# Gated linear attention of layer 0 set between the projection units of a two-layer diffusion block

## The chip, the cores and the metric

The kernel runs on one core of one Trainium2 chip, in one launch. The metric is the device time of that core in microseconds. Engines are named as in the profile: PE (TensorE), DVE (VectorE), ACT (ScalarE), POOL (GpSimd), SP (SyncE, which only issues transfers). Each engine runs its own instructions in the order written, and waits on semaphores for the others.

## The reference

Two transformer layers work on 512 tokens `x` and 256 context tokens `ctx` of width 1024, in float32. A conditioning vector gives six shift, scale and gate vectors for each layer (`silu(c) @ w_mod + b_mod`). Layer 0 has two mixers side by side:

```
aq, ak, av, bq, bk, bv, bo, rf, rb = split(h @ w_in)    # widths 512,128,128,256,256,512,512,16,16
log_f = log_sigmoid(rf @ gf_w + gf_b) / 16              # log_b likewise from rb
oa = window_attention(rope(aq), rope(ak), av, ...)      # 8 query heads, 2 key heads
ob = bidir_gla(bq * 64**-0.5, bk, bv, log_f, log_b)     # 4 heads, chunks of 64, both directions
y  = concat(oa, rms(ob) * norm_g * silu(bo)) @ w_out
# one direction of gla, per chunk:
cum = cumsum(log_a);  qg = q * exp(cum);  kg = k * exp(-cum)
o   = tril(qg @ kg.T) @ v + qg @ s_in
s   = exp(cum_last) * (s_in + kg.T @ v)                 # as the kernel arranges it
```

Then come a residual with gate and norm, a SwiGLU feed-forward (2816 wide) and its residual. Layer 1 has neighbourhood attention in place of the two mixers. Only `x` is returned.

## The kernel before, in words

**Precision.** Every large product is done in three passes of split float32: a weight tile `w` becomes `w_hi` (ACT, line 729) and `w_lo = w - w_hi` (POOL or DVE, line 454), the activations `h_hi` and `h_lo`, and PE adds hi*hi, hi*lo and lo*hi (`product3`, line 1451, and `tm_product`, line 1475). Small products are plain float32, and each of those matmuls shows as two records.

**Units.** `weight_units` lists all weights in the order in which PE uses them, 1024 columns at most to a unit. SP loads them into `w_raw` (3 places); ACT and POOL split them into rings of 3. ACT's and POOL's `feed(s)` split everything up to unit `s` at the place in their programs where it is written. An `fm_unit` is 24 passes over 512 and 256 columns with 128 output features on the partitions. `v0` (8 units, values for 6 token tiles) has the token on the partitions.

**Modulation.** A block of `w_mod` (one of 12 vectors) is eight rows of 512 KB. `modulation_rows` multiplies them (line 1519), ACT copies the result (`mod_copy`, line 738), PE turns it (`modulation_columns`, line 1532) and DVE adds the bias (`modulation`, line 1103). `modulation_plan` hangs the rows of blocks 2 to 5 on the projection units, three to a unit, and those of blocks 6 to 11 on feed-forward steps.

**Order on PE in layer 0.** `v0`; 14 projection units (four `a_q`, two `a_k` with each key head doubled, two `b_q`, two `b_k`, four `b_o`), with modulation rows between them; the first `scores` of attention; unit 14 (128 columns of which the 32 low-rank ones are used); window attention over 24 pairs of heads. After attention comes GLA, six token tiles and 12 chunks: `z` = low-rank times gate weights (line 1744), ACT's Abs, Exp and Ln, DVE's minimum (1290), running sums with a triangular matrix (1750), Exp twice (932, 933), products with `b_q` and `b_k` (1300, 1305), keys turned (1758), eleven state steps (1770 on PE, 1324 and 1328 on DVE), and for each tile scores (1784), masks (1341), outputs (1809, 1819), squares (718), root on POOL (625), norm (1367), turn (1795), gate (1352) and the split into `h_hi` and `h_lo`. Then `gate_rows(0, 2)` (1554) and the output product `out0L` (1475).

**Feed-forward.** `ffn_in` takes two units for each `j` of 11. ACT's part of step `j` is silu, a `feed`, `hid_hi`, a `feed`, the hook of `j`, then transfers of `w_mod` rows; PE's hook and modulation rows of step `j` stand behind its second unit.

Banks: `claim` makes PE wait for the readers of a PSUM bank, `read_by` names them.

Of the kernel before, what the change touches and what calls it, by code (L numbers as in the profile page):

```python
# [48 lines left out]
UNIT = 1024  # L49

# [35 lines left out]
def weight_units(a):  # L86
# [28 lines left out]
    for k in range(KT):  # L115
        tm(w, k, [(0, C_AV, AKV), (AKV, C_BV, BV)])
    begin("in0")
    parts = [[(0, C_AQ + j * P, P)] for j in range(4)]
    parts += [[(0, C_AK + 64 * j, 64), (64, C_AK + 64 * j, 64)] for j in range(2)]
    parts += [[(0, c + j * P, P)] for c, n in ((C_BQ, 2), (C_BK, 2), (C_BO, 4)) for j in range(n)]  # L120
    parts += [[(0, AB_IN - P, P)]]
    for part in parts:
        fm(w, part)
    rows("out0L", a["ab_w_out"][0], range(KT))
    rows("out0C", a["ab_w_out"][0], range(KT))
# [23 lines left out]
FENCE = 2600  # L149


def modulation_plan(start):
# [12 lines left out]
    spread("in0", range(11), 2 * KT, 6 * KT, lambda i: start["in0"] + i if i else start["v0"] - 2, 5)  # L165
    half = [start["fi0L", h] for h in range(2)]
    spread(("fi0L", 0), range(4, 10), 6 * KT, 8 * KT, lambda j: half[0] + 2 * j, 5)
# [41 lines left out]
def build(nc, a, out):  # L209
# [23 lines left out]
    with ExitStack() as ctx:  # L233
# [12 lines left out]
        with ExitStack() as early:  # L246
            sb("before", [P, D], scope=early)

            rel = sb("rel", [P, 2, 8, BIAS_RUN], scope=early)
        with ExitStack() as early:  # L250
            sb("before_mask", [P, 4 * D + 4 * P], scope=early)
            mask0 = sb("mask0", [P, 7 * P], scope=early)
# [5 lines left out]
        near_b = sb("near_b", [P, LT, 2 * P], BF16)  # L258
        tri = sb("tri", [P, 2, P])
# [21 lines left out]
        with ExitStack() as s0:  # L281
            par_rows = sb("par_rows", [P, 2, P], scope=s0)
            mask_in = sb("mask_in", [P, LT * 2 * P], scope=s0)
        with ExitStack() as s1:
            b_q = sb("b_q", [P, 2, TOK], scope=s1)
            b_k = sb("b_k", [P, 2, TOK], scope=s1)
            b_v = sb("b_v", [P, NT, BV], scope=s1)
            b_o = sb("b_o", [P, 4, TOK], scope=s1)
            r_t = sb("r_t", [33, TOK], scope=s1)
            gw = sb("gw", [33, 2 * BQK], scope=s1)  # L290
            with ExitStack() as s2:
                with ExitStack() as s3:
                    sb("fence1", [P, FENCE], scope=s3)
                    mod_early = sb("mod_early", [P, MOD_RING, UNIT], scope=s3)
                rope = sb("rope", [P, 4, SEQ], scope=s2)
                cos, sin, rope_t = rope[:, 0], rope[:, 1], rope[:, 2:4]
                a_q = sb("a_q", [P, 4, TOK], scope=s2)
                a_k = sb("a_k", [P, 2, TOK], scope=s2)
                a_v = sb("a_v", [P, NT, AKV], scope=s2)
                prob0 = sb("prob0", [P, 2, 2, 5 * P], scope=s2)  # L300
            with ExitStack() as s2:
                with ExitStack() as s3:
                    la = sb("la", [P, NT, 2 * BQK], scope=s3)
                kg_t = sb("kg_t", [P, NT, 2 * BQK], scope=s2)
                qg = sb("qg", [P, 4, TOK], scope=s2)
                kg = sb("kg", [P, 4, TOK], scope=s2)
                att_m = sb("att_m", [P, 2, 4 * P], scope=s2)
# [8 lines left out]
        with ExitStack() as s1:  # L316
# [6 lines left out]
            on1 = sb("on1", [P, 2 * P], scope=s1)  # L323
# [15 lines left out]
        mod_landed = [sem(f"mod_landed{i}") for i in range(MOD_RING + MOD_HOLD)]  # L339
        (consts_in, par_in, x_in, gw_zero, gw_in, rel_in, stored) = map(sem, (  # L340
            "consts_in", "par_in", "x_in", "gw_zero", "gw_in", "rel_in", "stored"))
        gl_av = sem("gl_av")
# [13 lines left out]
        at_b, v_mixed, mask0_in = sem("at_b"), sem("v_mixed"), sem("mask0_in")  # L356
# [36 lines left out]
        def in0_bank(i):  # L393

            return 4 if i == 14 else 2 * (i % 2)

# [8 lines left out]
        def mod_slot(m):  # L405

            if m < 2 * KT:
                return m % MOD_RING
            return MOD_RING + m % MOD_HOLD if m >= 6 * KT else MOD_RING - MOD_HOLD + (m - 2 * KT) % MOD_HOLD

        def mod_place(m):
            n = mod_slot(m)
            return mod_raw[:, n - MOD_RING, :] if n >= MOD_RING else mod_early[:, n, :]
# [17 lines left out]
        mod_first = set(range(2 * KT))  # L431
        mod_next = {}
        for phase in ("in0", ("fi0L", 0), ("fi0L", 1), "fi0C"):
            at = sorted(i for name, i in mod_hooks if name == phase)
            mod_first |= set(mod_hooks[phase, at[0]])
            mod_next |= {(phase, i): mod_hooks[phase, j] for i, j in zip(at, at[1:])}

        def row_place(b):

            return gate_b[:, b % 2, 0:256] if b < 6 else mod_row[:, b % 2, :]  # L440

        def mod_bank(b):
            return 6 + b % 2

        def column_bank(b):
            return b if b < 2 else 4 + b % 2
# [114 lines left out]
        def _(sync):  # L561
# [14 lines left out]
            for u, parts in enumerate(units):  # L576
                if u == sp("v0") + RAW:
                    for m in range(12, 2 * KT):
                        mod_load(sync, m)
                    for dst, src in ((mask_in[:], a["k_near"]), (tri[:].rearrange("p a n -> p (a n)"), a["k_tri"]),  # L580
                                     (cos, a["k_cos"]), (sin, a["k_sin"])):
                        sync.dma_start(dst, src).then_inc(consts_in, 16)
                if u == sp("in0") + 6:
                    sync.wait_ge(pre_lo, PRE["mix0"] + NT)
                    sync.dma_start(mask0[:], a["k_window"]).then_inc(mask0_in, 16)
# [6 lines left out]
                for layout, at, width, src in parts:  # L592
                    dst = w_raw[:, u % RAW, :]
# [13 lines left out]
        def _(pool):  # L607
# [30 lines left out]
            feed(sp("in0") + 14)  # L638
            for t in range(NT):
                root(gla_ssq[:, t, :], gla_ms[:, t, :], gla_rs[:, t, :], P, t, gl_ssq, gl_ms, gl_rs, 4)  # L640
            feed(sp("out0C") + RING - 2)
# [68 lines left out]
        def _(act):  # L710
# [169 lines left out]
            for t in range(NT):  # L880
                wait_tm(act, "v0", t, KT)
                act.activation(b_v[:, t, :], ps(t, 0, BV), ACT.Copy).then_inc(v_act, 1)

            def in0_unit(i):
                s = sp("in0") + i
                feed(s + RING - 2)
                act.wait_ge(w_used, s + 1)
                bl = in0_bank(i)
                bc = bl + 1
                lat, con = ps(bl, 0, SEQ), ps(bc, 0, CTX)  # L890
                if i == 6:
                    act.wait_ge(masks_done, 1)
                if i < 6:
                    dst = a_q[:, i] if i < 4 else a_k[:, i - 4]
                    act.activation(dst[:, SEQ:], con, ACT.Copy).then_inc(fe_act, 1)
                    return
                if i < 8:
                    dst, fn, scale = b_q[:, i - 6], ACT.Copy, SCALE
                elif i < 10:
                    dst, fn, scale = b_k[:, i - 8], ACT.Copy, 1.0  # L900
                elif i < 14:
                    dst, fn, scale = b_o[:, i - 10], ACT.Silu, 1.0
                else:
                    dst, fn, scale = r_t[0:32], ACT.Copy, 1.0
                    lat, con = ps(bl, 0, SEQ, 96, P), ps(bc, 0, CTX, 96, P)
# [3 lines left out]
            for i in range(14):  # L909
                in0_unit(i)  # L910
                if i in (3, 6, 8, 11):
                    mod_copy({3: 2, 6: 3, 8: 4, 11: 5}[i])
                for m in mod_next.get(("in0", i), ()):
                    mod_load(act, m)
            feed(sp("in0") + 14)
            attention(0, lambda: in0_unit(14))


            for t in range(NT):
                act.wait_ge(gl_z, t + 1)  # L920
# [1007 lines left out]
```

## Time and profile before

| | us |
|---|---|
| median of 3 runs (1890.68 to 1891.32) | 1890.8 |
| profiled execution | 1891.36 |
| its span, first to last instruction | 1889.6 |
| PE busy | 1751.4 |
| ACT, POOL, DVE busy | 660.2, 596.8, 547.1 |
| mean granted clock of PE | 0.967 of full |

Busy times are of one profiled execution. A granted clock of 1.0 is 2.4 GHz, 0.5 is 1.2 GHz; a figure between is a mean over a stretch. A timeline row gives the start, how long the group lasts, the engine, line, output and inputs, the count, and in brackets how long the engine was idle before it and what ended that.

### The profile page before, as it was taken

How to read it: one execution, taken by the hardware profiler on the slowest of the kernel's cores; microseconds unless marked ns; L12 is line 12 of the kernel's file. 1: busy time of each engine (PE TensorE's matmuls, PEld its weight loads, DVE VectorE, ACT ScalarE, POOL GpSimd, SP SyncE). 2: the span in 40 equal slices, each digit the busy share in tenths (PEclk: the TensorE clock that was granted, in tenths of full speed). 3: DMA queues.
4: the chain of work that ended last, by engine and by line, in shares of the span. 5: the costliest groups of instructions: out<-in, count | busy, mean ns of one | idle time of the engine just before them, and what ended most of it. 6: DMA issues, size and time to landing. Idle time of an engine off the chain costs nothing.

```text
span 1889.6 us, 26709 instructions
## 1 busy us (share of the span) xinstructions
PE 1751.4 (93%) x10718; PEld 1439.8 (76%) x10718; DVE 547.1 (29%) x1057; ACT 660.2 (35%) x1145; POOL 596.8 (32%) x426
## 2 busy tenths in 40 slices
PE   4899999777999999999999999999999799999996
PEld 2788877466777778777789887887787588788875
DVE  2221047641442101100376542002773411011103
ACT  3321256512453212222255434223773432222221
POOL 1222200013753343334230005332543344444442
PEclk8899999779999999999999999999999799999998
DMA  8246400002336424652465663623101133333331
GB/s 332 55 147 209 145 13 2 1 2 64 107 97 206 151 90 145 198 173 92 156 183 148 180 190 89 121 81 123 35 2 34 45 93 98 93 97 96 94 99 57
DMA packets 208150, 204.97 MB, mean 108 GB/s; under 512 B 10950, under 2 KB 179356, under 8 KB 208028
## 3 DMA queue, kind: packets, MB, share of 16 engines
q1 hardware_dynamic: 195064, 162.25, 28.6%
q10 hardware_dynamic: 12964, 41.01, 6.8%
q8 instruction: 86, 1.41, 0.3%
q14 instruction: 36, 0.29, 0.0%
HBM read 201.14 MB, written 2.10 MB: 108 GB/s over the span
## 4 chain that ended last, share of the span: by engine, by line
PE 63%; DVE 3%; ACT 2%; issue 2%; POOL 1%; DVEq 0%; ACTq 0%; POOLq 0%
PE ps L1451 34%; PE ps L1475 22%; PE ps L1612 2%; PE ps L1668 2%; PE ps L1633 2%; PE ps L1519 1%; ACT w_hi L729 1%; DVE x_res L513 1%; POOL w_lo L454 1%; DVE x_res L1080 0%; DVE full L1052 0%; DVE w_lo L454 0%; PE ps L1554 0%; ACT junk L718 0%; DVE h_lo L1058 0%
## 5 line engine op out<-in xcount | busy, mean ns | idle before, releaser
L454 POOL TENSOR_TENSOR w_lo<-w_raw,w_hi 128x1024 fp32r<-128x1024 f32 (+1 forms) x203 | 482.3, 2377 | 916.1 <-ACT w_hi L729 915.9
L1451 PE MATMUL ps<-h_hi,w_hi 128*128 128x512 f32 (+1 forms) x1520 | 505.7, 352 | 18.1 <-DVE w_lo L454 8.6
L1451 PE MATMUL ps<-h_hi,w_lo 128*128 128x512 f32 (+1 forms) x1520 | 500.9, 349 | 0.0
L1451 PE MATMUL ps<-h_lo,w_hi 128*128 128x512 f32 (+1 forms) x1520 | 499.8, 348 | 0.0
L729 ACT ACTIVATE w_hi<-w_raw 128x1024 fp32r<-128x1024 f32 (+1 forms) x277 | 288.9, 1044 | 382.8 <-PE ps L1475 363.3
L1451 PEld LDWEIGHTS ps<-h_hi,w_hi 128*128 128x128 f32 x1520 | 275.5, 190 | 70.2 <-issue 25.8
L1451 PEld LDWEIGHTS ps<-h_hi,w_lo 128*128 128x128 f32 x1520 | 275.2, 190 | 37.4
L1451 PEld LDWEIGHTS ps<-h_lo,w_hi 128*128 128x128 f32 x1520 | 275.1, 190 | 36.4
L454 DVE TENSOR_TENSOR w_lo<-w_raw,w_hi 128x1024 fp32r<-128x1024 f32 x74 | 98.6, 1332 | 270.6 <-ACT w_hi L729 270.4
L1135 DVE TENSOR_TENSOR hid_f<-silu_g,ps 128x512 f32<-128x512 f32 (+1 forms) x66 | 39.4, 597 | 398.3 <-PE ps L1451 398.0
L1475 PE MATMUL ps<-w_hi,hid_hi 128*128 128x512 f32 x440 | 138.3, 395 | 8.1 <-ACT mod_row L738 3.0
L1475 PE MATMUL ps<-w_hi,hid_lo 128*128 128x512 f32 x440 | 137.9, 395 | 0.0
L1475 PE MATMUL ps<-w_lo,hid_hi 128*128 128x512 f32 x440 | 137.9, 394 | 0.0
L790 ACT ACTIVATE hid_hi<-hid_f 128x512 fp32r<-128x512 f32 (+1 forms) x66 | 36.9, 560 | 249.7 <-DVE hid_f L1135 249.7
L1475 PE MATMUL ps<-w_hi,h_hi 128*128 128x512 f32 (+1 forms) x352 | 107.0, 386 | 15.6 <-POOL w_lo L454 5.0
L1475 PE MATMUL ps<-w_lo,h_hi 128*128 128x512 f32 (+1 forms) x352 | 105.3, 381 | 0.0
L1475 PE MATMUL ps<-w_hi,h_lo 128*128 128x512 f32 (+1 forms) x352 | 105.1, 381 | 0.0
L1475 PEld LDWEIGHTS ps<-w_hi,hid_hi 128*128 128x128 f32 x440 | 82.5, 188 | 28.6 <-issue 9.6
L1475 PEld LDWEIGHTS ps<-w_lo,hid_hi 128*128 128x128 f32 x440 | 82.9, 188 | 19.4
L1475 PEld LDWEIGHTS ps<-w_hi,hid_lo 128*128 128x128 f32 x440 | 82.9, 188 | 19.3
L786 ACT ACTIVATE silu_g<-ps 128x512 f32<-128x512 f32 (+1 forms) x66 | 34.5, 523 | 168.6 <-PE ps L1451 168.5
L1475 PEld LDWEIGHTS ps<-w_hi,h_hi 128*128 128x128 f32 x352 | 66.4, 193 | 30.7 <-issue 12.9
(179 smaller groups left out, 1695.0 us busy)
## 6 DMA issues: line engine op xcount, KB each, us to landing
w_raw<-in_w_ffn_in SPq DMA_DIRECT2D x132, 512.0 KB, 3.8
w_raw<-in_w_ffn_out SPq DMA_DIRECT2D x66, 512.0 KB, 3.6
mod_raw<-in_w_mod ACTq DMA_DIRECT2D x39, 512.0 KB, 5.1
w_raw<-in_na_w_in SPq DMA_DIRECT2D x32, 512.0 KB, 3.7
mod_early<-in_w_mod ACTq DMA_DIRECT2D x29, 512.0 KB, 4.7
mod_early<-in_w_mod SPq DMA_DIRECT2D x19, 512.0 KB, 10.4
w_raw<-in_ab_w_out SPq DMA_DIRECT2D x16, 512.0 KB, 3.6
w_raw<-in_ab_w_in SPq DMA_DIRECT2D x13, 512.0 KB, 4.1
```

The source lines that it names most:

```text
L454: eng.tensor_tensor(w_lo[:, u % RING, 0:width], w_raw[:, u % RAW, 0:width], w_hi[:, u % RING, 0:width].bitcast(F32), ALU.subtract).then_in ...
L513: eng.tensor_tensor(x_res[:, t, :], x_res[:, t, :], post_place(name, i), ALU.add).then_inc(post_x, 1)
L729: act.activation(w_hi[:, u % RING, 0:width], w_raw[:, u % RAW, 0:width], ACT.Copy).then_inc(w_hi_done, 1)
L786: act.activation(silu_g[:, f % 2, 0:width], ps(2 * (f % 2), 0, width), ACT.Silu)\
L790: act.activation(hid_hi[:, j * width:(j + 1) * width], hid_f[:, f % 2, 0:width], ACT.Copy)\
L1135: dve.tensor_tensor(hid_f[:, f % 2, 0:width], silu_g[:, f % 2, 0:width], ps(2 * (f % 2) + 1, 0, width), ALU.mult).then_inc(ff_full, 1)
L1451: mm = pe.matmul(o[0], sta(x, o), mov(y, o), start=first and n == 0, stop=last and n == 2)
L1475: mm = pe.matmul(o, act(x, k, t), w[y][:, c:c + n], start=k == 0 and (x, y) == ("hi", "hi") and first_in_bank(name, i, c), stop=k == n_uni ...
L1519: mm = pe.matmul(ps(bank, 0, 256, 32 * g, 32 * g + 32), c_pad[:, k, :], mod_place(m)[:, 256 * g:256 * g + 256], start=k == 0, stop=k == KT ...
L1612: mm = pe.matmul(ps(scores_bank(layer, p, x), at, at + width), q, kk[:, col:col + width], start=at % 512 == 0, stop=i == len(runs[x]) - 1, ...
L1633: mm = pe.transpose(ps(4 + x, j * P, (j + 1) * P), probs(p, x, j), ident[:])
L1668: mm = pe.matmul(ps(bank, at, at + P, 64 * x, 64 * x + 64), value_tile(p, x, j), turned_probs(layer, p)[:, x, j * P:(j + 1) * P], start=j ...
```

## The change

GLA runs between the projection units, in place of after attention. `projection_steps()` gives the list; PE carries out the steps of a slot behind the unit's last matmul. Unit order, low-rank columns, head pairing, buffers and banks follow from that.

```diff
+def projection_steps():
+    rows = {(0, 0): 3, (0, 1): 3, (1, 0): 2, (1, 1): 2, (2, 0): 2, (2, 1): 2, (3, 0): 2}
+    steps, m = {}, 3 * KT
+    for at, n in rows.items():
+        steps.setdefault(at, []).append(("rows", list(range(m, m + n))))
+        m += n
+    for at, names in {
+            (0, 0): (("z", 2), ("z", 3), ("columns", 2)), (0, 1): (("z", 4), ("z", 5)),
+            (1, 1): (("cum", 0), ("cum", 1), ("columns", 3)), (2, 0): (("cum", 2), ("cum", 3), ("cum", 4)),
+            (2, 1): (("cum", 5), ("kt", 0), ("kt", 1)), (3, 0): (("kt", 2), ("kt", 3), ("kt", 4)),
+            (3, 1): (("kt", 5), ("columns", 4)), (4, 0): (("ds", 0), ("ds", 1)), (4, 1): (("ds", 2), ("ds", 3)),
+            (5, 0): (("ds", 4), ("ds", 5)), (5, 1): (("ds", 6), ("ds", 7)), (6, 0): (("ds", 8), ("ds", 9)),
+            (6, 1): (("ds", 10), ("scores", 0))}.items():
+        steps.setdefault(at, []).extend(names)
+    steps = {(i, 1): steps.get((i, 0), []) + steps.get((i, 1), []) for i in range(7)}
+    for t in range(NT):
+        steps[7 + t, 1] = [("turn", t - 1)] if t else []
+        steps[7 + t, 1] += [("out", t)] + ([("scores", t + 1)] if t + 1 < NT else [])
+    return steps
...
-        tm(w, k, [(0, C_AV, AKV), (AKV, C_BV, BV)])
+        tm(w, k, [(0, C_AV, AKV), (AKV, AB_IN - 2 * RANK, 2 * RANK), (VR, C_BV, BV)])
...
+    parts = [[(0, c + j * P, P)] for c, n in ((C_BK, 2), (C_BQ, 2), (C_BO, 4)) for j in range(n)]
+    parts += [[(0, C_AK, P)]]
+    parts += [[(0, C_AQ + 64 * j, 64), (64, C_AQ + 64 * (j + 4), 64)] for j in range(4)]
...
-    spread("in0", range(11), 2 * KT, 6 * KT, ...)
-    spread(("fi0L", 0), range(4, 10), 6 * KT, 8 * KT, lambda j: half[0] + 2 * j, 5)
+    spread(("fi0L", 0), range(3, 11), 5 * KT, 8 * KT, lambda j: half[0] + 2 * j, 5)
...                                             # PE
+            pe.wait_ge(r_out, 2)
+            claim(2, 6)                         # then six tiles of r_tok turned into r_t
...
+            modulation_rows(range(2 * KT, 3 * KT))
...
+            gla_z(0)
+            gla_z(1)
+            for i in range(13):
+                bl = 2 * (i % 2)
+                claim(bl, bl + 1)
+                fm_unit(sp("in0") + i, [(ps(bl, 0, SEQ), 0, SEQ), (ps(bl + 1, 0, CTX), SEQ, CTX)],
+                        middle=lambda: in0_step(i, 0))
+                read_by((bl, bl + 1), (fe_act, i + 1), *([(fe_dve, i - 7)] if i >= 8 else []))
+                in0_step(i, 1)
             gla_turn(NT - 1)
+            pe.wait_ge(rope_done, 5)
+            attention(0, lambda first: first())
...                                             # PE, a state step: order of the loops
-                for m in range(4):
-                    for hh in range(2):
+                for hh in range(2):
+                    for m in range(4):
...                                             # PE, first feed-forward half
-                                             8: lambda: modulation_columns(6)}, "ffn0L")
+                                             6: lambda: modulation_columns(5), 9: lambda: modulation_columns(6)},
...                                             # ACT
+            for i in range(13):
+                feed(sp("in0") + i + 2)
+                if i == 1:                      # six Exp, six Ln, then
+                    mod_copy(3)
+                if i == 2:
+                    gla_decay(2)
+                    gla_decay(3)
+                    gla_decay(4)
+                if i == 3:
+                    mod_copy(4)
+                for m in in0_later.get((i, 0), ()):
+                    mod_load(act, m)
+                in0_unit(i)
+                if i >= 7:
+                    gla_square(i - 7)
+                if i == 1:
+                    gla_decay(0)
+                    gla_decay(1)
+                if i == 2:
+                    gla_decay(5)
+                for m in in0_later.get((i, 1), ()):
+                    mod_load(act, m)
...
-                   {3: ..., 7: lambda: mod_copy(6), 10: lambda: mod_copy(7)})
+                   {3: ..., 6: lambda: mod_copy(5), 9: lambda: mod_copy(6), 10: lambda: mod_copy(7)})
...                                             # POOL
-            feed(sp("in0") + 14)
             for t in range(NT):
+                feed(sp("in0") + 9 + t)
                 root(gla_ssq[:, t, :], ...)
+            pool.wait_ge(w_used, sp("out0L"))
+            for t in range(NT):                 # h_hi and h_lo of the GLA half, from b_o
+                pool.wait_ge(gl_full, t + 1)
+                pool.tensor_copy(h_hi[:, 4:8, cols], b_o[:, :, cols]).then_inc(gl_hi, 1)
+                pool.tensor_tensor(h_lo[:, 4:8, cols], ..., ALU.subtract).then_inc(gl_lo, 1)
...                                             # DVE, after the state steps
+            for t in range(NT):
+                if t:
+                    rotate(7 + t)
+                    gla_gate(t - 1)
+                if t + 1 < NT:
+                    gla_mask(t + 1)
+                gla_norm(t)
+                if t == 0:
+                    gla_gain(3)
+            gla_gate(NT - 1)
+            attention(0)
```

A slot is what stands between two units; the transposes of the keys (`kt`) begin in the slot behind unit 2. `z` uses banks 4 and 5 in turn, `cum` banks 4, 5, 4, 5, 6, 4, `kt` banks 5, 6, 4, 5, 6, 4, the state steps 4 to 7, scores 4 and 5, outputs 6 and 7, turns 4; projection units use banks 0 to 3. DVE replaces ACT's Abs by two operations on `z` (the minimum, and twice the minimum less `z`). SP loads rows 16 to 23 of `w_mod` ahead of unit 5 of `v0`, rows 24 to 33 ahead of the weights of projection units 1 and 3, and the rotation tables ahead of unit 11; ACT loads rows 34 to 39. Query heads `j` and `j + 4` now share a unit, so `a_k` needs one unit, and the rows of `ab_w_out` are loaded in that order, in two transfers for each of the first four units. The whole window mask is loaded with the other constants and held in bfloat16.

## Rows read from the trace of the kernel before

**Rows 1.** The page, part 1: busy us, share of span, instructions of PE.
```profile
PE 1751.4 (93%) x10718; PEld 1439.8 (76%) x10718; DVE 547.1 (29%) x1057; ACT 660.2 (35%) x1145; POOL 596.8 (32%) x426
```

**Rows 2.** View by stretches: from:to length, busy by engine, PEclk, DMA share, GB/s.
```profile
108.90:248.20 139.30, 138.25 (x946) 111.82 (x945) 21.15 (x47) 25.71 (x41) 31.10 (x13) 1.00 0.53 165
...
256.70:336.30 79.60, 76.94 (x809) 57.22 (x808) 56.30 (x197) 56.04 (x160) 0.00 (x0) 1.00 0.01 2
336.30:443.50 107.20, 70.87 (x654) 55.76 (x653) 53.69 (x140) 32.21 (x87) 9.04 (x13) 0.72 0.00 1
...
370.00:387.00 17.00, 11.92 (x174) 8.18 (x168) 14.91 (x40) 0.00 (x0) 0.00 (x0) 0.50 0.00 1
```

**Rows 3.** PE's waits, 100 to 450: total us, times, longest.
```profile
PE ps L1809 <- DVE b_q L1352: 7.9, 3, 2.8
```

**Rows 4.** Timeline of PE: attention's last matmuls, and the first of `out0L`.
```profile
335.72 0.64 PE L1680 MATMUL ps<-ident,sm 128*64 128x128 f32 x8
...
449.90 0.70 PE L1475 MATMUL ps<-w_hi,h_hi 128*128 128x512 f32 x2 [1.63 <-ACT gate_b L776]
```

**Rows 5.** Timeline, end of `v0` and projections: PE, VectorE, ScalarE.
```profile
107.84 0.50 PE L1475 MATMUL ps<-w_hi,h_hi 128*128 128x128 f32 x2
108.18 0.50 PE L1475 MATMUL ps<-w_lo,h_hi 128*128 128x128 f32 x2
...
109.06 1.28 DVE L1263 COPY a_v<-ps 128x128 f32<-128x128 f32 x6 [36.09 <-PE ps L1475]
...
117.43 1.50 PE L1519 MATMUL ps<-mod_early,c_pad 128*32 128x256 f32 x24
...
237.41 0.60 ACT L906 ACTIVATE b_o<-ps 128x512 f32<-128x512 f32 x1 [6.39 <-PE ps L1451]
...
245.96 0.60 ACT L906 ACTIVATE b_o<-ps 128x512 f32<-128x512 f32 x1 [6.72 <-PE ps L1451]
```

**Rows 6.** Timeline of the GLA stretch: ScalarE and PE.
```profile
344.42 0.60 ACT L923 ACTIVATE la<-ps 128x512 f32<-128x512 f32 x1 [0.45 <-PE ps L1744]
...
346.12 0.60 ACT L923 ACTIVATE la<-ps 128x512 f32<-128x512 f32 x1 [0.45 <-PE ps L1744]
...
348.69 3.78 ACT L928 ACTIVATE la<-la,one_col 128x512 f32<-128x512 f32 x6
...
350.19 3.61 PE L1750 MATMUL ps<-tri,la 128*128 128x128 f32 x16 [4.11 <-DVE la L1290]
...
357.26 2.14 PE L1750 MATMUL ps<-tri,la 128*128 128x128 f32 x16 [0.19 <-ACT kg L933]
...
400.88 2.05 PE L1809 MATMUL ps<-b_v,att_m 128*128 128x128 f32 x16
402.86 1.16 PE L1819 MATMUL ps<-state,qg 64*64 64x128 f32 x32
...
404.71 1.16 PE L1784 MATMUL ps<-qg,kg 64*128 64x128 f32 x16
```

**Rows 7.** Timeline of PE: one of the state steps, eight alike.
```profile
378.32 1.15 PE L1770 MATMUL ps<-b_v,kg_t 64*64 64x128 f32 x16 [0.50 <-DVE state L1324]
```

**Rows 8.** Timeline of PE: the last output and the last turn.
```profile
436.73 1.97 PE L1819 MATMUL ps<-state,qg 64*64 64x128 f32 x24
...
442.62 1.09 PE L1795 MATMUL ps<-ident,b_k 128*128 128x128 f32 x4 [3.27 <-DVE b_k L1367]
```

**Rows 9.** Timeline, start of attention: PE and ScalarE.
```profile
246.97 1.13 PE L1612 MATMUL ps<-a_k,a_q 64*128 64x256 f32 x8 [1.05 <-ACT b_o L907]
...
250.49 0.71 ACT L819 ACTIVATE prob<-prob,negm 128x512 f32<-128x512 f32 x1
...
256.71 1.13 PE L1612 MATMUL ps<-a_k,a_q 64*128 64x256 f32 x8
```

**Rows 10.** Timeline, end of the first feed-forward half: ScalarE and PE.
```profile
661.38 0.36 ACT L738 ACTIVATE mod_row<-ps 128x256 f32<-128x256 f32 x1
...
662.10 0.71 PE L1475 MATMUL ps<-w_hi,hid_hi 128*128 128x512 f32 x2 [2.96 <-ACT mod_row L738]
```

More of the change, by code:

```diff
@@ L220, in unit_width @@
     def unit_width(u):
-        return sum(width for _, _, width, _ in units[u]) * (KT if units[u][0][0] == "fm" else 1)
+        return sum(width for layout, _, width, _ in units[u] if layout != "bottom") * (KT if units[u][0][0] == "fm" else 1)
     def sp(name):
@@ L291, in build @@
+            a_v = sb("a_v", [P, NT, AKV], scope=s1)
             with ExitStack() as s2:
[L292 to L298, printed above, removed]
@@ L951, in _ @@
+            attention(0, lambda: None)
             gate_rows(0, 2)
@@ new lines, in _ @@
+            modulation(4)
+            dve.wait_ge(fe_act, 4)
+            dve.wait_ge(gl_dec, NT)
+            for n in range(NT):
+                cols = slice(GLA_TILES[n] * P, (GLA_TILES[n] + 1) * P)
+                for d in range(2):
+                    last = dve.tensor_tensor(qg[:, 2 * d:2 * d + 2, cols], qg[:, 2 * d:2 * d + 2, cols],
+                                             b_q[:, :, cols], ALU.mult)
+                last.then_inc(gl_q, 1)
+            for i in range(2 * NT - 1):
+                gla_state(i)
+                if i in (4, 8):
+                    gla_gain(i // 4 - 1)
@@ L1737, in _ @@
-            pe.wait_ge(rope_done, 6)
-            attention(0, lambda first: (first(), in0_unit(14)))
-            pe.wait_ge(gw_in, 64)
-            claim(*range(8))
-            for t in range(NT):
-                pe.matmul(ps(t, 0, 512), r_t[:, t * P:(t + 1) * P], gw[:], start=True, stop=True).then_inc(gl_z, 1)
-                read_by((t,), (gl_la, t + 1))
-            for t in range(NT):
-                claim(6 + t % 2)
-                pe.wait_ge(gl_la, t + 1)
+            read_by((6, 7), (v_dve, 2))
@@ L1822, in _, with gla_turn, in0_step @@
                 mm.then_inc(gl_o, 1)
-                read_by((ob, ob + 1), (gl_on, t + 1))
-                if t:
-                    gla_turn(t - 1)
+                read_by((6, 7), (gl_on, t + 1))
+            def gla_turn(t):
+                pe.wait_ge(gl_on, t + 1)
+                claim(4)
+                for h in range(4):
+                    mm = pe.transpose(ps(4, h * P, (h + 1) * P), gla_on[:, t % 2, h * P:(h + 1) * P], ident[:])
+                mm.then_inc(gl_f, 1)
+                read_by((4,), (gl_full, t + 1))
+            gla = {"z": gla_z, "cum": gla_cum, "kt": gla_keys, "ds": gla_change, "scores": gla_scores, "out": gla_out,
+                   "turn": gla_turn, "rows": modulation_rows, "columns": modulation_columns}
+            def in0_step(i, half):
+                for name, x in in0_steps.get((i, half), ()):
+                    gla[name](x)
+            gla_z(0)
+            gla_z(1)
+            for i in range(13):
[5 more added lines that the diff above has]
+                in0_step(i, 1)
             gla_turn(NT - 1)
+            pe.wait_ge(rope_done, 5)
+            attention(0, lambda first: first())
             gate_rows(0, 2)
```

465 lines of the change are left out of this document (244 added, 221 removed).

## The prediction, made before the result was known

> **What bounds the kernel now.** I read the page first: TensorE (PE) is busy 93% of the span [rows 1]. The reader should see there that only time in which PE waits, or work taken from PE, can shorten the kernel. The view by stretches then shows where PE waits [rows 2]. In the projections (108.9 to 248.2) PE is busy 138.25 of 139.3 us while VectorE has 21 us and ScalarE 26 us of work. In the stretch of gated linear attention (GLA, 336.3 to 443.5) PE is busy 70.87 of 107.2 us at a mean granted clock of 0.72. That is the only stage ahead of the feed-forward part with both a large gap and a low clock. The list of PE's waits names its gaps, the longest in total VectorE's `b_q` with 7.9 us in three times [rows 3]. They are the links of one dependent chain (logarithm, running sum, transpose, states, output), which nothing else covers. So the limit of that stage is latency, and the limit of its neighbour is PE.
>
> **The sum's frame.** I cut the profiled execution where the order of work changes. It took 1891.4 us, 1.8 more than its span of 1889.6. The median of the runs is 1890.8, so 0.6 less; a difference worked out on the first is carried to the second.
>
> **1. The stretch after attention goes.** Attention's last matmul for a norm ends at 336.36, and `out0L` starts at 449.90 [rows 4]: 113.5 us. Afterwards only `gate_rows(0, 2)` stands between them, 32 records of 128 columns. Such records take some 0.13 us each at the high clock (16 in 2.05 or 2.14 [rows 6]), so about 4.2. The wait for ScalarE's second gate copy, 1.63 us [rows 4], stays. Attention's last `h_lo` lies beside this. 113.5 - 5.8 = **107.7 us removed**. The GLA split of `h_hi`/`h_lo` moves from ScalarE and VectorE to GpSimd during attention, where GpSimd has no work at all in 79.6 us [rows 2]: six copies and six subtractions at no more than a `w_lo` subtraction of twice the size (13 in 31.10 us, 2.4 each [rows 2]) are under 29 us. Nothing if that cover holds; if it ran past the end, `out0L` would wait for it.
>
> **2. What the projections become.** From `v0`'s last matmul (108.86) to the second `scores` of attention (256.71) it is 147.85 us now [rows 5, 9]. The new PE program, term by term:
> - 13 units instead of 15. ScalarE's copies start at 237.41 and 245.96 [rows 5]: 8.55 us a unit. 13 x 8.55 = 111.2.
> - 24 modulation rows (blocks 2 to 4; block 5 leaves). Three of them take 1.50 us [rows 5]; with the change of shape I take 0.52 a row: 12.5. Eight stand bare before unit 0, sixteen in the slots behind units 0 to 3. Three transposes of columns: 0.8.
> - The low-rank columns. VectorE must copy banks 6 and 7 (four copies) before PE can turn them. `a_v` alone took 1.28 us in six copies [rows 5]; I take 1.7 of wait, bounds 0.5 and 2.5. Six matmuls of two records: 1.5. Together 3.2.
> - GLA's matmuls at the high clock. `z`: 1.70 us apart at the low clock (ScalarE's readers) [rows 6], half of that at the high one, 6 x 0.85 = 5.1. Running sums: 2.14 for two tiles, 6.4 in all. Transposes of `kg`: 24 records of 0.13, 3.1. Scores: 1.08 each, 6.5. Outputs: 1.98 + 1.08, two of them shorter, 18.0. Five turns of 0.6: 3.0. Total 42.1 [rows 6].
> - The eleven state steps. PE needs 1.15 us for one at a granted clock of 0.50 [rows 2, 7], so between 0.55 and 1.1 at the high one; the reordered loop changes row halves more often and column halves less, and no row shows what that does. With its wait of 0.50 for VectorE the step is 1.65 long [rows 7]: VectorE's pace, some 0.8 for each of its two halves. Four steps in a slot: PE's fourth must wait for VectorE's second sum, 0.6 + 0.1 + 3 x 0.8 = 3.1, then 0.65: 3.75 us. If a step cost 1.1, it would be 4.7. The slot behind unit 6 has three steps and the first scores, which need VectorE's last sum: 4.7 ahead of them. I take 3.75 + 3.75 + 4.7 = 12.2, bounds 11 and 15.
> - Waits in the slots. Behind unit 0, `z` 4 and 5 reuse banks 4 and 5 and wait for VectorE, which first does the modulation columns and then two passes a tile: 1.2 us. Behind unit 1 there is none: ScalarE's six Exp and six Ln (3.78 us for six [rows 6]) with two changes of table between them end some 15 us after unit 0, and the first running sum is wanted at 18.5. Behind unit 2, `cum` 5 and `kt` 0 and 1 reuse banks which ScalarE's two Exp a tile (about 1.0) free in 3.4, 4.4 and 5.5 us, while PE comes to them at 5.3, 6.4 and 6.9. That is where turning one unit later pays: keys 2 to 5 need VectorE's 1.6 us a tile. Behind unit 8 the third scores need `gla_gate(0)`, queued on VectorE behind `rotate` (six of them are most of VectorE's 21.15 us in the projections [rows 2], so under 3.5; I take 2.8): ready at 3.7, wanted at 3.7. 1.0 for what I miss: 2.2.
> - 13 changes of shape at 0.1: 1.3.
> - The tail. After the last output PE waits for the squares, GpSimd's root and VectorE's norm: 438.70 to 442.62, 3.9 us [rows 8]. Then turn 0.75, scores 1.13, and the first softmax, which unit 14 covered: scores end at 248.1 and the second Exp ends at 251.2 [rows 9]. Now PE meets that wait, about 1.9 us more than the unhindered order, and 1.5 for a lower clock after the pause (the turn at 442.62 took 1.09 us, 0.27 a record where 0.13 is the high clock's). 3.9 + 0.75 + 1.13 + 1.9 + 1.5 = 9.2.
>
> Sum 111.2 + 12.5 + 0.8 + 3.2 + 42.1 + 12.2 + 2.2 + 1.3 + 9.2 = 194.7, against 147.85: **46.8 us added**.
>
> **3. v0.** 32 more columns in 144 matmuls. A 512 and a 128 take 0.34 us together [rows 5]; a 512 and a 256 take 8.55 / 24 = 0.356. So 128 columns more cost 0.017, 32 of them 0.004: 0.6 us, and 0.2 for GpSimd's wider `w_lo`: **0.8 added** (bounds 0 and 2). SP's eight loads of block 2 come between the weights of `v0` units 4 and 5, which are wanted much later. The six loads issued behind `mod_used` hold up unit 3's weights on SP, which are not wanted for some 30 us.
>
> **4. The first feed-forward half.** Block 5's eight rows go there: 4.2, of which three rows fall into a wait that is there already, so 2.5. Then the hooks: PE turns columns 5 at `j` = 6 and columns 6 at `j` = 9, and ScalarE copies the row to be turned in its hook of the same `j`, behind silu's partner, `hid_hi` and a `w_hi`. The trace has this order once, at the end of the half: `mod_row` is copied from 661.38, and PE goes on at 662.10 after 2.96 us of wait [rows 10]. Twice that is 5.9. Bounds: 0 if ScalarE came early, which its in-order queue excludes, and 6.5. The columns 0.25, and 0.5 for rows whose loads ScalarE issues only after `pre_high`. **9.2 added.** The two records after that wait took 0.71 us, so no clock was lost in it.
>
> Total: -107.7 + 46.8 + 0.8 + 9.2 = **-50.9**. 1891.4 - 50.9 = 1840.5; on the medians **1840**.
>
> The clock is where the Trainium skill speaks against the change. The row: 370 to 387, short state matmuls between waits of 0.5 us ran at 0.50 of the full clock (1.2 GHz) [rows 2, 7]; attention, with matmuls as small but few waits, at 1.00 [rows 2]. The Trainium skill (TensorE: Matmul & The Clock Gate, section "HAM oscillation — how this bites in real kernels") says that bursts of matmuls parted by waits throw the engine back to the lower clock each time. By it every slot would start low, the third rival; by the attention row it would not, and the sum stands.
>
> **Rivals.**
> - *The waits come along.* PE's 36.3 us of gaps [rows 2] are not hidden but land in the slots, because a slot holds several dependent steps and PE is in order. For: slots 0 and 2 are tight. Against: the dependent steps stand a whole unit (8.55) apart. Two fifths of them would be 15 us: 1855.
> - *Cheaper.* The low-rank wait, the waits in the slots, the slow clock in the tail and part of the state chain are not met, and the column waits shrink: -9: 1831. For: all were taken at or above the middle. Against: the 2.96 was measured.
> - *Lower clock, slower than before.* The granted clock falls at each slot. The slots' 42.1 us of small matmuls then take up to 1.7 times as long (3.61 against 2.14 for two tiles [rows 6]), +29, the rows and states +8, and some 4 us at the head of each of 13 units run at half pace, +26: 1840 + 63 = 1903. It decides from about 50 us, that is, only if nearly all slots fall. Against: PE would be busy almost without a gap from 68 to 336.
> - *The chain slips a slot.* ScalarE holds `feed` behind a wait for PE, and a unit starts without its weights. A `w_hi` (1.06) and `w_lo` (2.4) after the late wait is 3.7 us, in eight units 30: 1870. Against: weights are fed two units ahead.
>
> **How the numbers follow.** Forecast 0.58, its own range 1834 to 1848; waits 0.19; cheaper 0.15; slipping chain 0.05; low clock 0.03. The range of 8 in 10 takes the forecast, most of the cheap case and the middle of the waits: 1832 to 1858. A measurement tells 0.2% (3.8 us) from no change: faster 0.96, within 0.2% 0.01, slower 0.03.
>
> **What would show it.** Right: 13 units of 8.55 us and slots of 3 to 8 us between them, clock 1.00 through `v0`, projections and attention; `out0L` about 6 us after attention; two new waits of about 3 us for `mod_row` at `j` = 6 and 9; a pause of about 4 us before the last turn. Wrong: waits over 2 us in the slots behind units 1 to 5, a clock below 1.00 there, a wait for `w_lo` at a unit's start, or `out0L` waiting for GpSimd.

## The result, and the profile after

The changed kernel takes 1860.0 us (median of 4 runs, 1858.07 to 1861.23); the kernel before took 1891.1 beside it. The ratio is 0.9835, 95% interval 0.9818 to 0.9852. I forecast 1840 with a range of 1832 to 1858: the direction was right, the gain of 51 us was 31, and the time lies above the range.

The view by stretches of the changed kernel (from:to length, busy us by engine, PEclk, DMA share, GB/s):

```profile
109.20:117.40 8.20, 6.80 (x81) 4.26 (x81) 3.02 (x8) 1.83 (x3) 0.38 (x1) 1.00 0.36 112
117.40:230.00 112.60, 100.30 (x771) 80.02 (x771) 51.54 (x115) 32.16 (x51) 19.20 (x8) 0.94 0.35 100
230.00:306.00 76.00, 72.12 (x634) 63.31 (x632) 29.50 (x61) 17.58 (x61) 18.85 (x17) 1.00 0.14 36
306.00:311.60 5.60, 3.13 (x13) 1.94 (x13) 2.87 (x8) 0.07 (x1) 5.36 (x7) 0.50 0.00 0
311.60:392.70 81.10, 78.88 (x808) 58.67 (x808) 57.49 (x198) 56.71 (x162) 5.73 (x7) 0.97 0.01 2
392.70:399.20 6.50, 3.84 (x33) 3.71 (x33) 0.88 (x3) 3.19 (x5) 0.00 (x0) 1.00 0.01 1
```

The 107.2 us stretch at a clock of 0.72 [rows 2] has no counterpart: attention ends at 392.7 and `out0L` begins 6.5 us later, where it was 113.5 [rows 4]. That row of the sum held. The second row is the one to dwell on: PE stands idle 12.3 of 112.6 us, at 0.94 of the clock, where it had stood idle 1.05 in 139.3 at 1.00 [rows 2]. The waits of PE say for whom (total us, times, longest):

```profile
PE ps L1871 <- DVE state L1370: 5.3, 4, 3.4
PE ps L1886 <- DVE state L1370: 4.9, 1, 4.9
PE ps L1918 <- DVE gla_on L1395: 3.8, 1, 3.8
...
PE ps L1827 <- DVE a_v L1329: 1.5, 1, 1.5
```

The last two I had forecast (3.9 and 1.7). The first two, the state steps and the first scores behind them, I had at 5 to 6 together (12.2 less eleven steps of 0.55 to 0.65), and they are 10.2. PE's timeline over the slots behind units 4, 5 and 6:

```profile
184.56 1.18 PE L1871 MATMUL ps<-b_v,kg_t 64*64 64x128 f32 x32
186.25 0.69 PE L1871 MATMUL ps<-b_v,kg_t 64*64 64x128 f32 x16 [0.51 <-DVE state L1368]
187.90 0.69 PE L1871 MATMUL ps<-b_v,kg_t 64*64 64x128 f32 x16 [0.96 <-DVE state L1370]
197.19 1.18 PE L1871 MATMUL ps<-b_v,kg_t 64*64 64x128 f32 x32
198.88 0.69 PE L1871 MATMUL ps<-b_v,kg_t 64*64 64x128 f32 x16 [0.50 <-DVE state L1370]
202.95 0.69 PE L1871 MATMUL ps<-b_v,kg_t 64*64 64x128 f32 x16 [3.38 <-DVE state L1370]
213.63 1.18 PE L1871 MATMUL ps<-b_v,kg_t 64*64 64x128 f32 x32
...
220.95 2.08 PE L1886 MATMUL ps<-qg,kg 64*128 64x128 f32 x16 [4.94 <-DVE state L1370]
...
233.54 1.95 PE L1898 MATMUL ps<-b_v,att_m 128*128 128x128 f32 x16
```

The slots behind units 4 and 5 hold the same four steps, yet the fourth waits 0.96 in one and 3.38 in the other. After the 3.38 the unit takes 10.0 us (203.64 to 213.63) and not 8.55, and after the 4.94 the scores take 2.08 where they took 1.16 [rows 6]: the lower clock follows both long waits. It does not need a long one. PE's timeline behind unit 0:

```profile
132.06 1.12 PE L1839 MATMUL ps<-gw,r_t 33*128 33x512 f32 x2 [0.81 <-DVE la L1339]
...
135.85 0.84 PE L1546 MATMUL ps<-h_hi,w_hi 128*128 128x512 f32 x2
```

Behind waits of 0.81 and 0.20 (at 133.39) a pair of matmuls of unit 1 takes 0.84 where the high clock gives 0.51, and unit 1 takes 10.1 us (134.44 to 144.56). VectorE and GpSimd beside the state steps:

```profile
187.79 1.95 DVE L1374 TENSOR_TENSOR state<-state,decay 128x256 f32<-128x256 f32 x2
...
199.44 2.70 DVE L1409 TENSOR_SCALAR b_o<-b_o,par_col 128x768 f32<-128x768 f32 x1
...
215.88 2.70 DVE L1409 TENSOR_SCALAR b_o<-b_o,par_col 128x768 f32<-128x768 f32 x1
...
221.61 0.62 DVE L1409 TENSOR_SCALAR b_o<-b_o,par_col 128x768 f32<-128x768 f32 x1
```
```profile
186.56 2.55 POOL L497 TENSOR_TENSOR w_lo<-w_raw,w_hi 128x1024 fp32r<-128x1024 f32 x1 [8.03 <-ACT w_hi L793]
199.19 2.53 POOL L497 TENSOR_TENSOR w_lo<-w_raw,w_hi 128x1024 fp32r<-128x1024 f32 x1 [10.08 <-ACT w_hi L793]
215.63 2.53 POOL L497 TENSOR_TENSOR w_lo<-w_raw,w_hi 128x1024 fp32r<-128x1024 f32 x1 [13.91 <-ACT w_hi L793]
```

The gain (line 1409) lasts 2.70 us twice and 0.62 once, and each long one overlaps a `w_lo` of GpSimd. So does the decay product of 1.95 (line 1374). The second surprise is in the first feed-forward half, PE's timeline (only modulation rows and turns, and the first matmuls behind):

```profile
521.02 1.91 PE L1641 MATMUL ps<-ident,xs 128*128 128x128 f32 x16
...
528.94 2.79 PE L1616 MATMUL ps<-mod_raw,c_pad 128*32 128x256 f32 x24 [6.01 <-DVE full L1113]
531.66 0.80 PE L1546 MATMUL ps<-h_hi,w_hi 128*128 128x512 f32 x1
532.25 0.63 PE L1546 MATMUL ps<-h_lo,w_hi 128*128 128x512 f32 x1
...
572.07 0.55 PE L1629 MATMUL ps<-ident,mod_row 128*128 128x128 f32 x2 [2.75 <-ACT mod_row L802]
572.55 2.79 PE L1616 MATMUL ps<-mod_raw,c_pad 128*32 128x256 f32 x24
...
614.47 0.41 PE L1629 MATMUL ps<-ident,mod_row 128*128 128x128 f32 x2 [2.75 <-ACT mod_row L802]
614.81 1.50 PE L1616 MATMUL ps<-mod_raw,c_pad 128*32 128x256 f32 x24
```

The two waits of 2.75 are those forecast from [rows 10]. The 6.01 is not: right behind the turns of the context tokens (521.02), the first modulation row waits for a VectorE operation. From `out0L`'s start to the end of that half it was 212.2 us before and is 231.2 now: 19.0 more, where I had 9.2.

### The profile page after: what moved, and what is told of

Read it like the earlier page. It is cut to its first block, busy times and chain, and to the rows that moved or that the text cites. A ratio compares the mean times of both kernels' runs of the same rounds, so it can differ in the third digit from the quotient of the medians.

```text
span 1859.4 us, 26540 instructions
## 1 busy us (share of the span) xinstructions
PE 1726.9 (93%) x10634; PEld 1419.4 (76%) x10634; DVE 558.7 (30%) x1059; ACT 651.7 (35%) x1130; POOL 604.1 (32%) x436
## 4 chain that ended last, share of the span: by engine, by line
PE 65%; DVE 4%; ACT 3%; issue 2%; POOL 1%; ACTq 0%; DVEq 0%; POOLq 0%
PE ps L1546 35%; PE ps L1572 22%; PE ps L1709 2%; PE ps L1765 2%; PE ps L1730 2%; PE ps L1616 1%; ACT w_hi L793 1%; DVE x_res L556 1%; POOL w_lo L497 1%; DVE full L1113 0%; DVE x_res L1141 0%; DVE h_lo L1119 0%; ACT full L817 0%; DVE w_lo L497 0%; PE ps L1651 0%
## 5 line engine op out<-in xcount | busy, mean ns | idle before, releaser
L1546 PE MATMUL ps<-h_hi,w_hi 128*128 128x512 f32 (+1 forms) x1488 | 500.1, 355 | 18.2 <-DVE w_lo L497 8.5
L1546 PE MATMUL ps<-h_hi,w_lo 128*128 128x512 f32 (+1 forms) x1488 | 494.3, 351 | 0.0
L1546 PE MATMUL ps<-h_lo,w_hi 128*128 128x512 f32 (+1 forms) x1488 | 493.7, 350 | 0.0
L1572 PEld LDWEIGHTS ps<-w_hi,hid_hi 128*128 128x128 f32 x440 | 83.0, 190 | 27.3 <-issue 8.3
```

What stands on the lines that cost most here:

```text
L1546: mm = pe.matmul(o[0], sta(x, o), mov(y, o), start=first and n == 0, stop=last and n == 2)
L1572: mm = pe.matmul(o, act(x, k, t), w[y][:, c:c + n], start=k == 0 and (x, y) == ("hi", "hi") and first_in_bank(name, i, c), stop=k == n_uni ...
```

## The experiments

Each kernel is the changed one with the edit shown. Times are medians; all were timed beside the kernel before (1891.0 to 1891.4). Up to the turns of the low-rank columns the changed kernel and the ten runs have the same order of work, and these turns begin at 108.9 to 110.6 in the eleven traces. So a microsecond or so of a total is not the edit's, and I also give what the stretch around each edit gained, from its trace.

**Context turns one step earlier** (`x1_turn2`).

```diff
-                   {3: lambda: [pre_high("ffn0C", i, C_TILES) for i in range(CT)], 6: ...    # ACT
+                   {2: lambda: [pre_high("ffn0C", i, C_TILES) for i in range(CT)], 6: ...
-            ffn_in(..., {3: lambda: pre_rest("ffn0C", C_TILES, scaled=2), ...                 # DVE
+            ffn_in(..., {2: lambda: pre_rest("ffn0C", C_TILES, scaled=2), ...
-            ffn_in(..., {3: lambda: pre_turn("ffn0C", range(CT)), ...                         # PE
+            ffn_in(..., {2: lambda: pre_turn("ffn0C", range(CT)), ...
```

> The changed kernel with the context tokens' normalisation for the feed-forward (PE's turns, ScalarE's and VectorE's parts) one step earlier, at j = 2 for j = 3; nothing else moves. Theory A (bank): the 6.01 us at 528.94 is block 5's first modulation row waiting for bank 7, which the turns of j = 3, issued just before it, have filled. Then the wait goes whole, and with it the slower clock behind it (24 records in 2.79 for 1.50, seven matmuls at some 0.43 for 0.23): -6.0 - 1.3 - 1.5 = -8.8 us, 1851. Theory B: the wait is for the data of that step (VectorE or the transfer of the row) and only moves: 0 to -2 us.

1849.7 us, 10.3 less. The rows at `j` = 3 run without a wait and at full pace:

```profile
508.59 1.91 PE L1641 MATMUL ps<-ident,xs 128*128 128x128 f32 x16
521.35 1.50 PE L1616 MATMUL ps<-mod_raw,c_pad 128*32 128x256 f32 x24
```

Theory A holds: it was the bank and not the row's data, which was there when PE came at 521.35. From `out0L`'s start to the end of the half it is 220.9 us where it was 231.2, again 10.3 less: 8.7 at this place, and 1.6 because the wait of 2.75 at 561.83 is followed by rows at 1.50 in this trace, where those at 572.55 had taken 2.79. These 1.6 are not the bank's.

**Turns of columns 5 and 6 one step later** (`x2_cols`).

```diff
-             6: lambda: modulation_columns(5), 9: lambda: modulation_columns(6)},
+             7: lambda: modulation_columns(5), 10: lambda: modulation_columns(6)},
```

> The changed kernel with PE's turns of modulation columns 5 and 6 one step later (j = 7 and 10 for 6 and 9), ScalarE's copies left where they are. Theory A (same-step hand-over): each turn waited 2.75 us for ScalarE's copy of the same step; now the copy is a step old: -5.5, and -1.3 to -2.5 for the lower clock seen behind the first: 1852 to 1853. Theory B: PE is ahead of ScalarE anyway and meets the wait at the next hand-over between them: 0 to -2 us.

1853.5, 6.5 less: theory A, both waits (5.5 together) gone and none in their place. The half takes 223.5 us for 231.2; of the 2.2 beyond the waits 1.6 are the lower clock that had followed the first.

```profile
580.44 0.38 PE L1629 MATMUL ps<-ident,mod_row 128*128 128x128 f32 x2
580.75 1.50 PE L1616 MATMUL ps<-mod_raw,c_pad 128*32 128x256 f32 x24
```

**GpSimd's `w_lo` held back** (`x4_lolate`).

```diff
+                    late = {sp("in0") + 7: (gl_s, 8), sp("in0") + 8: (gl_s, 16), sp("in0") + 9: (bo_done, 3)}
+                    if fed[0] in late:
+                        pool.wait_ge(*late[fed[0]])
                     if not by_dve[fed[0]]:
                         low_part(pool, fed[0])
```

> The changed kernel, GpSimd's w_lo of units 7, 8 and 9 held back until VectorE has done its states 3, 7 and its third gain; VectorE's program is unchanged. Theory P (shared port): VectorE's b_o gain took 2.70 us twice because GpSimd's w_lo ran beside it, and 0.62 the third time, alone. Then all take 0.62, PE's waits of 3.38 and 4.94 shrink by 2.1 each, the decay product at 187.79 takes 0.76 for 1.95: -4.2 us, 1856. Theory Q: the gain is slow for a reason of its own (it waits for ScalarE's silu, its 768 columns): durations as they are, 0 us. If the held-back w_lo makes a unit start late, a wait for w_lo shows in front of unit 7, 8 or 9.

1852.2, 7.8 less. VectorE's program is the same, and its gain now takes what it takes alone:

```profile
186.41 0.76 DVE L1377 TENSOR_TENSOR state<-state,decay 128x256 f32<-128x256 f32 x2
...
198.07 0.61 DVE L1412 TENSOR_SCALAR b_o<-b_o,par_col 128x768 f32<-128x768 f32 x1
...
211.03 0.62 DVE L1412 TENSOR_SCALAR b_o<-b_o,par_col 128x768 f32<-128x768 f32 x1
```
```profile
PE ps L1874 <- DVE state L1373: 3.2, 4, 1.3
PE ps L1889 <- DVE state L1373: 2.9, 1, 2.9
```

Theory P, and Q falls. The waits shrank by 2.1 and 2.0 (5.3 and 4.9 before the edit), as expected. The time fell by 3.6 us more than that: the output behind unit 7 starts 41.1 us after VectorE's first state copy (183.97 to 225.10), where it was 48.2 (185.34 to 233.54), 7.1 less with 4.1 of waits. The other 3.0 are the lower clock: it no longer follows the shorter first wait (1.3 us), which gives unit 6 back 1.4; behind the second, of 2.9, it comes later, so that the scores take 1.16 for 2.08 and unit 7 loses 0.6 less. It does still come there: at 215.91 a pair of matmuls takes 0.84.

**Gains behind the states** (`x5_gains`).

```diff
             for i in range(2 * NT - 1):
                 gla_state(i)
-                if i in (4, 8):
-                    gla_gain(i // 4 - 1)
-            gla_gain(2)
+            for j in range(3):
+                gla_gain(j)
```

> The changed kernel, VectorE's gains 0 and 1 moved behind the eleven state steps; GpSimd unchanged. Theory P: the gains leave the chain but the decay product now meets w_lo. Slot 5: the sum that frees the bank starts at once, -2.65. Slot 6: the decay product is held some 1.5 us, -1.1. Together -3.7 us, 1856, a decay product of about 2 us in each slot, and gains of 0.62 each. Theory Q: slots 5 and 6 lose 2.7 us each, -5.4, the decay products stay at 0.76, the gains at 2.7.

1852.1, 7.9 less, again twice what I had expected, but the signature is P's: the decay product now pays in the gain's place, about 2 us in each of the three slots, and three gains together take 1.67.

```profile
198.24 1.94 DVE L1374 TENSOR_TENSOR state<-state,decay 128x256 f32<-128x256 f32 x2
...
210.86 1.93 DVE L1374 TENSOR_TENSOR state<-state,decay 128x256 f32<-128x256 f32 x2
...
214.36 1.67 DVE L1409 TENSOR_SCALAR b_o<-b_o,par_col 128x768 f32<-128x768 f32 x3
```

The waits fell by what P had said: the longest of the state steps from 3.4 to 1.0, that of the scores from 4.9 to 3.7. The same stretch (183.18 to 224.78) takes 41.6 where it was 48.2: 6.6 less with 3.7 of waits, the rest again the clock. In this trace PE also kept the high clock in unit 1, which the edit does not touch; it fell there in the traces of all seven other kernels that have the steps only at the end of units.

**Loops of the state step as before** (`x6_dsorder`).

```diff
-                for hh in range(2):
-                    for m in range(4):
+                for m in range(4):
+                    for hh in range(2):
```

> The changed kernel with the loops of a state step on PE back in the order of before (column halves inside, m outside). Theory A (clock only): the 1.15 us a step of before were the low clock, half of it at the high one; the steps stay near 0.57 (two in 1.18), 0 us. Theory B (order): alternating row halves lets neighbours overlap, without it a step takes up to 1.1: two in 2.2, and as VectorE's pace hides the rest, some +0.5 in each of three slots, +1.5 us.

1860.2, and two steps take 1.18 in either order:

```profile
187.69 0.84 PE L1546 MATMUL ps<-h_lo,w_hi 128*128 128x512 f32 x2
...
197.23 1.18 PE L1871 MATMUL ps<-b_v,kg_t 64*64 64x128 f32 x32
...
202.96 1.15 PE L1871 MATMUL ps<-b_v,kg_t 64*64 64x128 f32 x16 [3.38 <-DVE state L1370]
```

Theory A. The rows decide it; the four times (1858.5 to 1863.3) could hide the 1.5 us of theory B. What I had bounded from 0.55 to 1.1 is 0.59 a step, and the low clock alone made it 1.15, as in the last row. The first row shows something else: behind unit 4 the waits are those of the changed kernel (0.49 and 0.97 for 0.51 and 0.96), yet here the clock fell behind them and there it did not.

**Steps in the middle and at the end of a unit** (`x7_halves`).

```diff
-    steps = {(i, 1): steps.get((i, 0), []) + steps.get((i, 1), []) for i in range(7)}
```

> The changed kernel without the line that merges each unit's two groups of steps: for units 0 to 6 the first group stands in the middle of the unit, the second at its end. ScalarE, VectorE, GpSimd and SP are unchanged. Theory A (pieces at the end only cost waits): two state steps in half a unit (4.3 us) never wait for VectorE's 1.65 a step; PE's waits of 5.3, 0.5 and 4.9 us fall to 2 or so, the low clock behind them goes (some 3.5 us): -11 us, 1849. Theory B: ScalarE's and VectorE's steps are late by more than half a unit, so that the waits reappear inside units 1 to 3, with changes of shape: -3 to +5 us.

1842.2, 17.8 less, more than the 11 of theory A, and of its kind. PE's timeline: two state steps at a time, five times, without a wait, and one wait ahead of the scores. The stretch over them shows a clock of 1.00:

```profile
182.47 1.18 PE L1870 MATMUL ps<-b_v,kg_t 64*64 64x128 f32 x32
188.01 1.18 PE L1870 MATMUL ps<-b_v,kg_t 64*64 64x128 f32 x32
193.55 1.18 PE L1870 MATMUL ps<-b_v,kg_t 64*64 64x128 f32 x32
...
206.22 1.16 PE L1885 MATMUL ps<-qg,kg 64*128 64x128 f32 x16 [0.91 <-DVE state L1369]
```
```profile
184.50:216.00 31.50, 30.59 (x270) 25.61 (x269) 19.72 (x40) 3.63 (x6) 7.72 (x3) 1.00 0.30 68
```

The waits of 5.3, 0.5 and 4.9 became 0.9; the waits for `z` and a modulation copy (1.0 and 0.5) went too: 11.3 us. From the low-rank turns to the output behind unit 7 it is 105.6 us where it was 122.9 (110.60 to 233.54), 17.3 less. The other 6.0 are the clock but for some tenths: in the changed kernel it had cost 1.5 in unit 1, 1.4 in unit 6, 0.9 in the scores and 2.0 in unit 7, and in this trace it does not fall between `v0` and the last turn.

**The halves with `w_lo` held back** (`x11_halves_lolate`): both edits above.

> The halves, with GpSimd's w_lo of units 7, 8, 9 held back as in the earlier run. Theory: with two state steps at a place no decay product stands in PE's way, so the 2 us decay products beside w_lo (three in the halves' trace) cost PE nothing, and taking the contention away gives under 1 us. Rival: what held-back w_lo gave before (8 us) was mostly its own doing, and comes again: 3 us or more.

1843.2 against 1842.2. All eleven decay products take 0.76, where two had taken 2.0 in the halves' trace (not three, as I had counted), and the third gain takes 0.61, where it had taken 2.74 beside `w_lo`. From VectorE's first state copy to the output behind unit 7 it is 36.0 us for 36.1, so nothing is gained: here the slowed instructions cost nothing, because PE does not wait for them.

**Output 5 in the middle of unit 12** (`x8_tail`).

```diff
+    steps[6 + NT, 0] = steps.pop((6 + NT, 1))            # turn 4, out 5
...                                                       # ACT: gla_square(5) before in0_unit(12)
...                                                       # DVE, t = 5: gate 4, norm 5, then rotate
-                if t:
+                if t and t < NT - 1:
                     rotate(7 + t)
+                if t:
...
+            rotate(6 + NT)
             gla_gate(NT - 1)
             attention(0)
```

> The changed kernel with turn 4 and output 5 in the middle of unit 12 in place of behind it; ScalarE's squares of tile 5 ahead of its part of unit 12, VectorE's gate 4 and norm 5 ahead of its last rotation. Theory: the 3.83 us wait for the last norm hides beside the second half of unit 12; the last rotation, 2.8 us, then stands ahead of attention's first scores in its place. Turns of attention's first pair come 6.6 us after unit 12's end where it is 13.5 with 3.5 of work moved ahead: -3.4 us, 1856.5. Rival: turn 4 in the middle waits for norm 4 (late by VectorE's mask), and the gain is 0 to -1.

1855.9, 4.2 less. The turn follows the unit at once, and the last rotation takes the norm's place in front of the scores:

```profile
301.20 0.60 PE L1923 MATMUL ps<-ident,gla_on 128*128 128x128 f32 x4
305.00 1.13 PE L1714 MATMUL ps<-a_k,a_q 64*128 64x256 f32 x8 [3.20 <-DVE a_q L1427]
307.63 2.08 PE L1714 MATMUL ps<-a_k,a_q 64*128 64x256 f32 x8 [1.49 <-DVE raw_max L1232]
```

So the places changed as the theory has it, but its size is not shown. From the output behind unit 7 to `out0L` it is 164.4 us for 165.6 in the changed kernel, 1.2 less. Another 2.8 of the profiled execution lie between `out0L` and the end of the feed-forward half, where the waits are the same and the clock happened to fall less (the row behind the first wait of 2.75 takes 1.50).

**All edits at the end of units** (`x9_all`: `x1`, `x2`, `x4`, `x5` and `x8` together).

> The changed kernel with all five edits: context turns one step earlier, the turns of columns 5 and 6 one step later, w_lo held back, gains behind the states, tail in the middle of unit 12. If the causes are separate places on PE's path, they add: -10.3 (bank, as measured), -6.5 (columns, as measured), -8 (port and clock, as measured) and 1 more for both edits of it, -3.4 (tail): -29 us, 1831. If two of them shared one wait, less: above 1836.

1832.7, 27.3 less where 29 was the sum: nearly separate places. By the traces the states' part gives 9.3 (to the output behind unit 7), the stretch to `out0L` 1.7 and the feed-forward half 16.5. The tail gives half of the 3.4 that I had added for it.

**The best version** (`x10_best`: `x7`, `x1`, `x2` and `x8`).

> The halves (first group of each unit's steps in its middle), context turns at j = 2, turns of columns 5 and 6 one step later, and the tail in the middle of unit 12. If the four are separate places on PE's path, their measured gains add: 1842.2 - 10.3 - 6.5 - 4.2 = 1821 us. If the halves already gave part of what another edit gives, above 1825.

1825.2 us (1823.18 to 1825.84); ratio to the kernel before 0.9642, interval 0.9617 to 0.9667. It beats both kernels, by 66 and 35 us. It is 4 us short of the sum of its parts (1821). The traces say where: 17.3 are gained before the output behind unit 7, as by the halves alone, 16.4 in the feed-forward half, as in `x9_all`, but only 0.6 at the tail, for which I had added 4.2. Its largest waits in that half of the kernel are 3.2 for the last rotation and 2.2 for `xs`.

## Why the prediction was wrong

The steps in order, from the spans (1889.6 to 1859.4, 30.2 us, where I had 50.9), each rounded:

| step | forecast | measured |
|---|---|---|
| after attention: removed | 107.7 | 107.1 (113.5 to 6.5) |
| attention itself | 0 | +1.4 |
| projections and head of attention | +46.8 | +54.8 |
| `v0` | +0.8 | +0.1 |
| first feed-forward half | +9.2 | +19.0 |
| the rest | 0 | +1.5 |

**The mechanism and its largest term were right**: the stretch went whole, units of 8.55 us, modulation rows, `z`, running sums, transposes, outputs and the tail each came within about a microsecond of their terms, together 3.4 below. Beside the projections PE did not fall to the lower clock at every slot, but it did at three of thirteen slots, behind the two long waits and behind the short ones after unit 0: the third rival happened in small, for 5.8 us. Two of my signs of being wrong came with it, a wait over 2 us behind unit 5 and a clock below 1.00. No projection unit waited for its weights.

**Step 4 failed, +9.8.** I priced the moved rows by their PE time and by the wait of [rows 10], and looked at what they wait for in transfers, but not at the bank that they claim. Block 5 sums in bank 7, its first row now stands behind the turns of the context tokens, which fill banks 4 to 7, and a `claim` in an in-order engine stops everything behind it. In the kernel before, the first rows of that half came at `j` = 4, after the readers were done. The price was 6.0 of wait, 1.3 on the rows and 1.5 on the matmuls behind them at the lower clock, 8.8 of the 9.8; moving the turns gave back 8.7 at that place. My sentence that no clock is lost in such a wait failed as well: it held for one wait of 2.96 and not for the one at 572.07, whose rows took 2.79 for 1.50 (1.6 with the matmuls behind them). The waits themselves were right (2.75 for 2.96).

**In step 2 the term of the state steps was mis-sized.** I had 12.2 with an upper bound of 15; the three slots took 4.0, 6.45 and 7.3 to the scores, 17.8, and the lower clock in units 6 and 7 and in the scores added 4.3. Unit 1 added another 1.5 by the clock. The sum had put the lower clock in the slots and behind them at nothing, and left it to a rival of 63 us or none. One reason is that I took VectorE's 1.65 us a step from a stretch in which GpSimd did nothing: GpSimd was busy 9.04 of 107.2 us there [rows 2], none of it beside the states. Beside the projections GpSimd makes a `w_lo` for every unit, and in the three slots with states it starts 2 us into the slot (186.56, 199.19, 215.63), just when the slot's steps need VectorE. The row that I used was measured with the other engine silent. The other is that I left `gla_gain` out of the chain, where it stands twice; alone it costs 0.62, beside `w_lo` 2.70. With it a sum starts 3.3 us after the decay product before it (198.77 to 202.06), without it 0.9 (202.84 to 203.70): 2.4 more, twice, most of the 5.6 by which the three slots are longer.

The Trainium skill has this (SBUF — State Buffer, section "Who interferes with whom"): VectorE and GpSimd arbitrate for one port pair, which is locked for a whole instruction, and VectorE wants it in the fast modes of `tensor_scalar` and, beside a GpSimd instruction that reads SBUF as `w_lo` does, for a product of two SBUF operands. The runs agree in each point: the gain (`tensor_scalar`) and the decay product (two SBUF operands) were blocked, 2.70 for 0.62 and 1.95 for 0.76, and the sum `state + ps`, with one operand in PSUM, took 0.75 throughout, beside `w_lo` or not.

**Attention's 1.4 us**: its first turns and scores ran at the lower clock, 0.50 from 306.0 to 311.6 and on to about 316, which I had put into the tail once and not behind it. In the trace of `x7_halves` the clock was back before the second scores (293.94, in 1.13 for 2.08), and attention took 79.9 us for 81.1, where it was 79.7 before. The 1.5 us of the rest I have not traced.

**The range** was too narrow for what was left out. Its upper end came from one rival, waits in the slots, and none of the rivals was "a moved step claims something that its new neighbour holds".

## What to carry to other kernels

For each step that is moved, list what it claims (banks, buffers, slots) and who holds that at the new place; a price of its own work is not enough. A duration taken from a stretch in which another engine was idle is a lower bound for a stretch in which it is not: look up what GpSimd does beside each VectorE instruction on the chain. And where a chain between engines has a fixed pace, spread its steps no closer than that pace: two state steps every half unit never waited, four every unit did, and each microsecond of wait taken away gave back another 0.7 to 0.8 in clock (3.0 with 4.1, 2.9 with 3.7). When a time moves by more than its waits, compare the stretch around the edit in both traces before crediting the edit: at the tail 4.2 us by the medians were 1.2 at the place.

## What the runs showed of the hardware that I had not expected

One `tensor_scalar` of 128 x 768 takes 0.62 us alone and 2.70 beside GpSimd's subtraction of 2.5 us. 64 x 64 matmuls took the same time in either order of row and column halves (two steps of 32 records in 1.18). A single wait of 2.96 us of PE left the clock high at 662 in the kernel before, and waits of 2.75 in the changed one left it low once (records at 572.55 in 2.79) and high once (614.81 in 1.50): the same wait, two outcomes. In `x1_turn2` and in `x8_tail` both left it high. Short waits can do it too: 0.81 and 0.20 ahead of unit 1, and 0.49 and 0.97 ahead of unit 5 in `x6_dsorder`, were followed by the lower clock. What decides between the outcomes these runs do not show.
